# Sixteen late modulation sums move from the recurrence into the projection stage of a two-block mixer kernel

## The reference, cut to what matters

```python
def first_block(x, c, ctx, c_ctx, ...):
    shift, scale, gate = jnp.split(jax.nn.silu(c) @ w_ada[layer] + b_ada[layer], 3, axis=-1)
    ...
    h = rmsnorm(x, norm_g[layer]) * (1.0 + scale[:, None]) + shift[:, None]
    u = h @ w_in[layer]                        # 512 rows; uc = hc @ w_in for 256 context rows
    ya_c, ya = gdn_mixer(uc[..., :GDN_COLS], u[..., :GDN_COLS], ...)     # gated delta, 8 heads of 128
    yb_c, yb = rwkv_mixer(uc[..., GDN_COLS:], u[..., GDN_COLS:], ...)    # RWKV-7, 16 heads of 64
    x = x + gate[:, None] * (jnp.concatenate([ya, yb], axis=-1) @ w_out[layer])
    return rmsnorm(x, final_norm_g)
```

## Time and profile before

| | us |
|---|---|
| median of three runs | 3387.04 |
| profiled execution | 3392.42 |
| span of its trace | 3390.7 |
| TensorE busy | 2961.2 (87%) |
| VectorE busy | 1998.7 (59%) |
| ScalarE busy | 1032.4 (30%) |
| GpSimd busy | 712.0 (21%) |

### The profile page before, as it was taken

How to read it: one execution, slowest core, us unless ns; L and a number is a source line. 1 busy time by engine, 2 the same in 40 slices (tenths; PEclk the granted TensorE clock), 3 DMA queues, 4 the chain that set the end, 5 groups by cost and what they waited for, 6 DMA issues and landing times. The chain is left out here.

```text
span 3390.7 us, 71127 instructions
## 1 busy us (share of the span) xinstructions
PE 2961.2 (87%) x30422; PEld 2485.3 (73%) x30422; DVE 1998.7 (59%) x3450; ACT 1032.4 (30%) x1668; POOL 712.0 (21%) x526
## 2 busy tenths in 40 slices
PE   5999999989999938788878688878979999998896
PEld 2688888868888737777777687766867778785484
DVE  5465465555555426677776557863242999996223
ACT  3345465443333302222222123321023444413102
POOL 0000000000000002222222100007853344473383
PEclk8999999989999969999999679998989999999998
DMA  9424434435545445555565334417332222221331
GB/s 395 170 75 149 132 117 149 134 118 167 180 154 187 126 128 176 174 179 180 178 188 181 105 121 126 131 56 265 95 120 84 81 81 75 81 93 44 130 99 68
DMA packets 265224, 465.80 MB, mean 137 GB/s; under 512 B 108224, under 2 KB 156576, under 8 KB 258544
## 3 DMA queue, kind: packets, MB, share of 16 engines
q1 hardware_dynamic: 213152, 364.71, 33.0%
q0 software_dynamic: 20672, 67.27, 6.2%
q10 hardware_dynamic: 31120, 29.72, 2.8%
HBM read 382.60 MB, written 81.63 MB: 137 GB/s over the span
## 5 line engine op out<-in xcount | busy, mean ns | idle before, releaser
L1152 PE MATMUL pjl<-high,w_high 128*128 128x512 f32 x816 | 324.5, 398 | 29.2 <-DVE low L2792 16.4
L1154 PE MATMUL pjl<-high,w_low 128*128 128x512 f32 x816 | 319.9, 392 | 0.0
L1153 PE MATMUL pjl<-low,w_high 128*128 128x512 f32 x816 | 319.7, 392 | 0.0
L3220 DVE SCALAR_TENSOR_TENSOR arena<-arena,par 128x512 f32<-128x512 f32 x232 | 293.0, 1263 | 6.8
L2188 POOL DMA_DIRECT2D arena_r<-in_w_ada x256 | 137.5, 538 | 570.1 <-DVE arena_r L2572 476.1
L1135 POOL TENSOR_TENSOR w_low<-ring_o,w_high 128x1024 fp32r<-128x1024 f32 x88 | 226.8, 2577 | 6.9
L2862 POOL TENSOR_TENSOR w_low<-ring_o,w_high 128x1024 fp32r<-128x1024 f32 x64 | 169.3, 2646 | 250.1 <-ACT w_high L3049 249.7
L1133 POOL TENSOR_TENSOR w_high<-ring_o,cst 128x1024 fp32r<-128x1024 f32 x88 | 174.0, 1977 | 213.5 <-PE pjl L1154 66.0
L1283 DVE TENSOR_TENSOR wl_in<-ring,wh_in 128x1024 fp32r<-128x1024 f32 x136 | 164.1, 1220 | 86.5 <-ACT wh_in L1276 86.4
L1264 PE MATMUL xu<-h_high,wh_in 128*128 128x512 f32 x512 | 207.9, 406 | 0.0
L1152 PEld LDWEIGHTS pjl<-high,w_high 128*128 128x128 f32 x816 | 154.6, 189 | 72.6 <-issue 27.0
(11 more groups left out here) (508 smaller groups left out, 7015.5 us busy)
## 6 DMA issues: line engine op xcount, KB each, us to landing
ring<-in_w_lr SPq DMA_DIRECT2D x136, 512.0 KB, 4.3
arena_r<-in_w_ada POOLq DMA_DIRECT2D x256, 256.0 KB, 3.8
arena_p<-in_w_ada SPq DMA_DIRECT2D x32, 1024.0 KB, 8.5
ring_o<-in_w_out SPq DMA_DIRECT2D x64, 512.0 KB, 3.7
ring_o<-in_w SPq DMA_DIRECT2D x64, 512.0 KB, 3.7
arena_r<-rk_d SPq DMA_DIRECT2D x47, 384.0 KB, 5.0
rk_d<-arena_p SPq DMA_DIRECT2D x72, 192.0 KB, 1.9
arena_p<-gate_rows SPq DMA_DIRECT2D x32, 386.0 KB, 6.2
```

Source lines behind the costliest of these rows:

```text
L1152: pe.matmul(lat, wh[:, c], ah, start=kk == 0, stop=False)
L1153: pe.matmul(lat, wh[:, c], al, start=False, stop=False)
L1154: last = pe.matmul(lat, wl[:, c], ah, start=False, stop=kk == KT - 1)
L3220: link(dve.scalar_tensor_tensor(ca[:], x[:, o:o + LAT], w[:, o:o + 1], ca[:], ALU.mult, ALU.add))
```

## The change

The late products leave the recurrence and go to the projection stage. `later(n)` now does the next `n` products, in places written out by hand: 6, 6 and 4 in the front (one block), 16 in each of the eight pairs in groups of 2, 1, 2, 1, 2, 2, 3 and 3, and 16 for each of seven heads: 3, 3, 2, 2 in `head` and 2, 2, 2 in the `next_head` before. GpSimd issues the reads there (`late_reads`) into two buffers instead of four: read `x` waits for product `x - 2`. The accumulator is one block, used anew for every block; its partition sums (`late_columns`, four products) and bias (`late_kept`) follow in the same pair or head. In the pair `late_columns` stands in front of the bonus product, in the head inside the last tile, behind the squares' sums. To make room, `VX` and ScalarE's copies into it are gone, and TensorE turns the values in twice as many products of 64 rows; TensorE's loop over the pairs is written out; a constant table that nothing reads (`lmask`) is gone. The delta recurrence loses its partition sums and bias additions.

```diff
@@ front_vector
             parts(2)
+            later(6)
             weights(6)
             row(6)
+            later(6)
             weights(7)
             row(7)
+            later(4)
             mods(3)
@@ delta_core, rest of TensorE, VectorE
-                if 1 < n:
-                    if n == 2:
-                        pe.wait_ge(S["r_lu"], 256)
-                    for q in range(4 * n - 8, 4 * n - 4):
-                        last = pe.matmul(shares[:, q:q + 1], acc[:, q // 4, q % 4 * P:q % 4 * P + P], ones[:, 0:1], start=True, stop=True)
-            last.then_inc(S["g_sh"], 1)
...
-            dve.wait_ge(S["g_sh"], 1)
-            dve.tensor_tensor(gate[:], shares[:, 0:KT], ...)
-            dve.tensor_tensor(mod2[:], shares[:, KT:64], ...).then_inc(S["g_md"], 1)
@@ the recurrence: buffers, table and reads
-LATE = 4
-LATER = {0: 1, 2: 1, 3: 1, 4: 2, 5: 1, 6: 1, 8: 1, 9: 1, 13: 2, 14: 2, 15: 1, 16: 1, 17: 1}
...
-            for x in range(256):
-                if x >= LATE:
-                    pool.wait_ge(S["r_lu"], x - LATE + 1)
-                pool.dma_start(late[:, x % LATE], io["w_ada"][8 + x // 16, :, x % 16]).then_inc(S[f"r_lw{x % LATE}"], 16)
@@ the projection stage: reads and partition sums
+    def late_reads(pool, x0, x1):
+        for x in range(x0, x1):
+            if x >= 2:
+                pool.wait_ge(S["p_lu"], x - 1)
+            pool.dma_start(late[:, x % 2], io["w_ada"][8 + x // 16, :, x % 16]).then_inc(S[f"p_la{x % 2}"], 16)
+
+    def late_columns(pe, cols, due):
+        pe.wait_ge(S["p_lu"], due)
+        for c in range(4):
+            last = pe.matmul(cols[:, c:c + 1], acc[:, c * P:c * P + P], ones[:, 0:1], start=True, stop=True)
+        last.then_inc(S["p_lr"], 1)
...
+            late_reads(pool, 0, 16)
             front_pool(pool)
+            late_reads(pool, 16, 256)
@@ turn_values, values_in
-                pe.wait_ge(S["p_vx"], i * 4 + 2 * n + 2)
+                pe.wait_ge(S["p_mv"], i + 1)
                 for c in range(6):
-                    last = pe.matmul(ctxs[0][:, 64 * c:64 * c + 64], VX[:, c], istk, start=True, stop=True)
+                    at = 384 * n + 64 * c
+                    last = [pe.matmul(ctxs[0][hs, 64 * c:64 * c + 64], v[hs, at:at + 64], istk[hs], start=True, stop=True)
+                            for hs in (slice(0, 64), slice(64, P))]
...
-            def values_in(i, n):
-                act.wait_ge(S["p_mv"], i + 1)
-                for h in range(2):
-                    act.activation(diag(VX, h), chunked(v, h)[:, 6 * n:6 * n + 6], ACT.Copy).then_inc(S["p_vx"], 1)
@@ TensorE, head and pair
                 turn_norms(h + 1)
+                late_columns(pe, head_cols, 16 * h + 160)
                 tile(t, 3, False, (1,))
...
                 pe.wait_ge(S["p_rk"], i + 1)
+                late_columns(pe, pair_cols, i * 16 + 32)
                 pe.matmul(up[0][:, 0:LAT], blk, kds, start=True, stop=True).then_inc(S["p_bs"], 1)
...
-            with pe.Fori(0, PAIRS - 1) as i:
-                period(i, False)
-            period(PAIRS - 1, True)
+            for i in range(PAIRS):
+                period(i, i == PAIRS - 1)
@@ VectorE, next_head, head and pair
                 head_conv(h, 0)
+                if h:
+                    later(2)
                 head_silu(h, 0)
...
                 head_conv(h, 1)
                 if h:
+                    later(2)
                     weights(m + 7)
+                    later(2)
                 head_silu(h, 1)
...
+                if h:
+                    late_kept(8 + h)
                 if more:
                     weights(m + 2)
+                    later(3)
                     weights(m + 3)
+                    later(3)
                 dve.wait_ge(S["q_nl"], 48 * (h + 1))
...
                 if more:
                     weights(m + 4)
+                    later(2)
                     weights(m + 5)
+                    later(2)
                     next_head(h + 1, m)
...
                 sums(i, 0)
+                later(2)
                 weights(m + 2)
+                later(1)
                 weights(m + 3)
+                later(2)
                 streams(i, 0)
+                later(1)
                 weights(m + 4)
+                later(2)
                 weights(m + 5)
+                later(2)
                 sums(i, 1)
+                later(3)
                 weights(m + 6)
+                later(3)
                 streams(i, 1)
...
                 dve.wait_ge(S["p_bs"], i + 1)
+                late_kept(i + 1)
@@ the product itself, and the bias
+            def later(n):
+                for x in range(x_[0], min(x_[0] + n, 256)):
+                    m, k = x // 16, x % 16
+                    which = 0 if m < 4 else 2
+                    c = csk[:, 3 * k + which:3 * k + which + 1]
+                    dve.wait_ge(S[f"p_la{x % 2}"], x // 2 * 16 + 16)
+                    if k == 0:
+                        if m:
+                            dve.wait_ge(S["p_lr"], m)
+                        dve.tensor_scalar(acc, late[:, x % 2], c, None, ALU.mult).then_inc(S["p_lu"], 1)
+                    else:
+                        dve.wait_ge(S["p_lu"], x)
+                        dve.scalar_tensor_tensor(acc, late[:, x % 2], c, acc, ALU.mult, ALU.add).then_inc(S["p_lu"], 1)
+                x_[0] += n
...
+                dve.wait_ge(S["p_lr"], m + 1)
...
-                    later(m, 3 * j)
                     dve.wait_ge(S["r_sa"], m * 12 + 2 * j + 2)
                     dve.tensor_copy(SA[j % 2][:], SA_).then_inc(S["r_sac"], 1)
                     fill(3 * j + 1)
-                    later(m, 3 * j + 1)
```

76 lines of the change are left out of this document (26 added, 50 removed).

## The result

The changed kernel takes 3535.96 us (median of four runs, 3528.11 to 3538.81) against 3388.26 for the kernel before: a ratio of 1.0428, with a 95% interval of 1.0402 to 1.0454. It is 148 us slower. I had forecast 64 us slower, and a range that ended at 3525. The sign was right, the size was not: the cost in the projection stage was 270 us where I had 165.

A forecast was written before the change was run, and what follows sets the result against it. TensorE bounds the projection stage, a chain of TensorE, ScalarE and VectorE the recurrence. Costs 10 + 62 + 71 + 22 = 165 us less 101 give +64 on 3392.4: 3456, or 3451 for a median; range 3370 to 3525.

The forecast's parts named there:

- What bounds the stages: Projection stage bound by TensorE, VectorE's order fixed; recurrence a chain where TensorE waits 117.2 us for three VectorE operations.
- The gain: Recurrence and the sums behind it: time given back once the late products leave, 101 us.
- my 94 us: Recurrence: 84 us of TensorE's waits and 10 us of clock won back.
- the fourth rival: Recurrence: the trip through DRAM takes its place, only 50 + 7 us come back; 3495 us, chance 0.12.
- The cost: Projection stage: front 10, eight pairs 62, seven heads 71, clock 22; 165 us in all.
- waits for reads, with the clock behind the stops: Projection stage: the part of the cost from products waiting for data and TensorE's low clock, 148 us.
- the products and partition sums themselves: Projection stage: cost without any waits for data, 2 + 2 + 13 us.
- I take 3.5: Projection stage, two buffers: 3.5 us from a product's end to use of the read it releases; ends 3.3 and 4.5.
- my third rival: Projection stage: reads collide with ring loads and stores, a turn takes 4.5 us; 3521 us, chance 0.15.
- Traffic on others: Projection stage: slowing of other transfers by the new reads; no term in the forecast, 0 us.
- The clock: Projection stage: TensorE loses 1.5 us to low clock behind each of 15 stops; 22 us, at most 38.
- The first rival: Projection stage: two buffers are enough, reads arrive in time, VectorE's idle time holds all products; 3303 us median, chance 0.10.

The follow-up runs named there:

- The kernels that take the change apart: The changed kernel (3536.0 us); with products not waiting for reads (3360.5); with reads also left out (3308.8); with no late sums (3265.7).
- the longer filler: Changed kernel with 25 (pairs) or 29 (heads) useless TensorE products in front of each of 15 long waits: 3508.8 us.
- the kernels with filler: Changed kernel with useless TensorE products before its 15 long waits: 18 (pairs) and 20 (heads), 3536.7 us; 25 and 29, 3508.8 us.
- the spread ones: Changed kernel with all 256 products and two buffers, products placed apart: 3423.7 us; with groups behind the bonus product cut down: 3352.3 us.
- the last spread kernel: Changed kernel with products placed apart and smaller groups behind the bonus product, still two buffers: 3352.3 us.

## Why the prediction was right in kind and wrong in size

- What bounds the stages: right. VectorE's order decides, TensorE stops for L2008's successor and for the heads' squares, 15 times. The recurrence gives back what its waits show.
- The gain: 101 forecast, 128 measured in the spans (111 + 12 + 5). L2604 is waited for 22.6 us instead of 80.9, and the granted clock of the recurrence is 0.98, where it was 0.93; this is that stretch in the changed kernel, with the same columns:

```profile
1532.00:2067.50 535.50, 476.49 (x15160) 462.13 (x15160) 279.76 (x969) 129.54 (x281) 0.00 (x0) 0.98 0.31 86
```

  I had let a denser chain win 10 of 36 us there, and TensorE's busy time fell by 35. But the same recurrence took up to 17 us more in other kernels, so that my 94 us for it are not shown to be wrong. The trip through DRAM, the fourth rival, took little: in the recurrence TensorE's waits for the addition behind it rose from the first row, before, to the second, after.

```profile
PE tp L2287 <- DVE arena_r L2524: 11.4, 4, 7.3
```

```profile
PE tp L2321 <- DVE arena_r L2558: 23.9, 13, 6.9
```

- The cost: 165 forecast, 270 measured. This is the step that failed, in its sizes and in one term that I put at nothing. The kernels that take the change apart (the stage ends at 1450.7, 1268.8, 1215.5 and 1182.1 us) divide it:

| part of the cost, us | forecast | measured |
|---|---|---|
| waits for reads, with the clock behind the stops | 148 | 182 |
| what the reads do to other transfers | 0 | 53 |
| the products and partition sums themselves | 17 | 33 |

- The same by pieces of the path, as means over seven pairs and seven heads of the changed kernel. The pieces are those of my count:

| piece, us | forecast | measured |
|---|---|---|
| pair: to the end of the first streams | 24.0 | 25.3 |
| pair: from there to the second scans | 11.8 | 15.2 |
| pair: from the scans to the end of L2018 | 21.0 | 21.3 |
| pair: from TensorE's restart to the next reciprocal | 16.0 | 19.2 |
| head: to the start of L1970 | 12.7 | 13.4 |
| head: from there to the convolutions | 18.1 | 20.5 |
| head: from there to the second sigmoid's product | 20.4 | 21.0 |
| head: from TensorE's restart to the next head | 16.4 | 20.3 |

- The pieces with the waits for reads are off by 1.6 us in a pair and 1.4 in a head, 23 us in all. Those that wait for stores are off by 3.4 and 2.4, 44 us. Those behind the stops are off by 3.2 and 3.9, 53 us, of which I had 22 as clock; with the longer filler these pieces are 16.0 and 17.4 us. The front is off by 7. So the largest miss is the stores, which had no term at all. That the reads make them late is seen where no product waits: the piece from L1970 to the convolutions takes 20.3 us there with the reads and 17.2 without them.
- "I take 3.5" for the turn: the mean was 4.2 in the pairs and 4.5 in the heads. I took a value near the shortest that I had seen, with a median landing of 3.8 us in the earlier trace rows under my eyes. The 3521 us of my third rival, with a turn of 4.5 us, were the nearest of all the figures, and I gave it 0.15. That they are near is in part luck: its cost of 229 us is 41 too low and its gain of 95 us is 33 too low, and the two errors cancel.
- Traffic on others: not priced. I let the reads collide with the ring's loads and the stores in the rival, and then only as a longer turn. What they do to the stores of the streams and heads (4.4 us to land instead of 1.6 in a pair; 6.4 instead of 4.0 for a head's 512 KB) had no term. In the pairs the kernel with unwaited products loses only 1.7 us to it, since the slack of 10 us is free there; in the changed kernel the slack is used up and the 3 us count in full. So a part of the 182 us above is traffic as well, and these runs do not divide it further.
- The clock: 1.5 us for a stop of 7 to 10; the trace has 3.4 behind the one in the pair above, and taking the stops away gave 27 us. I scaled the loss with the length of the stop. It doesn't scale: behind 4.75 us the sums are as slow as behind 11.73.
- The first rival, two buffers without waits: 3303 forecast. With the reads running and no product waiting for them the time is 3360, so the rival as I put it is 57 us too low; without reads it is 3309. VectorE's idle time holds all the products, but for 33 us in the stage where I had 17. My 17 us had the partition sums in the heads and in the front; in the pairs, where they take 0.95 us each, it had 2 us for all eight.
- The Trainium skill (Trainium Kernel Development and Optimization, Best Practices) says to double-buffer to overlap transfers with work. By these runs two buffers do that with one placement of the products (3352 us) and not with another that has groups of three to six in front of what TensorE needs (3536 us).
- By the Trainium skill (DMA: Bandwidth & Descriptors, Anatomy of one DMA) such a read takes 2.0 us plus its 256 KB at 436 GB/s, an estimate of 2.6 us. The trace has 2.8 at least and 3.5 in the median. Its lower price would have made my forecast worse.

## What to carry to other kernels

Before work moves into another engine's idle time, set the longest run of it against the number of its buffers: each time the run comes round to its first buffer again it waits for the rest of a turn, from "buffer free" to "data there", taken at its mean or above and not at its best. Then ask where the wait stands: with 230 us of waits in one placement the stage ended at 1264 us, as early as with products that never wait (1269), and with 235 us in front of what the bounding engine needs it ended 182 us later than that. Give a term of its own to what the new transfers do to the transfers that are already there, and another to what each stop costs behind it. A steep price can be shared: part of the work in each of two stages was faster (3320) than all of it in either (3388 and 3352).

## What the runs showed of the hardware

- TensorE at half clock behind short stops. In the kernels with filler, the spread ones and the one whose products don't wait, eight passes took 0.95 to 1.05 us behind stops of up to 2.36 us, anything from 1.05 to 1.87 behind 2.4 to 4.4 us, and 1.63 to 1.87 behind 4.46 us and more; behind 11 to 14 us it was 1.87. A longer stop did not make the eight passes behind it slower.
- Reads from GpSimd's queue landed in 3.3 us in the median in the pairs of the changed kernel and in 3.8 in its heads, against 3.8 in the recurrence before; with the products of the last spread kernel it was 4.0 and 4.7. They make SyncE's stores slower, from 4.0 to 6.4 us for 512 KB. It goes the other way too: in the recurrence, without the reads, the blocks that come back from DRAM (24 KB) landed in 2.3 us instead of 3.6, which may be a part of what the recurrence gave back.
- What stays open: how the stage's 53 us of traffic divide between late stores and late ring loads, which landed (850 to 1250 us) in 4.8 us in the median with the reads and in 3.8 without them. No run held the one and not the other. Why the recurrence is 15 us longer in one kernel than in another with the same queues. And the gain by itself: the kernel before without its late sums was not measured, so that what the recurrence gave back is known only together with the change's other edits.
